# Modulation units spread over the first product and the down products, and first units of two projections loaded to places of their own, in a two-block transformer kernel

## What the reference computes, cut to what matters

```
h = h + short_conv_mixer(rms_norm(h), a_w_in, a_conv, a_w_out)      # layer 0
h = h + swiglu(rms_norm(h), f_w_gu, f_w_down)
h = h + nsa_mixer(rms_norm(h), b_w_qg, b_w_o, shared_kv(h))         # layer 1
h = h + swiglu(...)
x = rms_norm(h)
mod = silu(c) @ w_ada + b_ada        # 1024 x 6144, the modulation
sh1, sc1, g1, sh2, sc2, g2 = split(mod, 6)
h = rms_norm_2(x) * (1 + sc1) + sh1 ;  proj = h @ w_in   # "qkv" begins it
...
```

## Time and profile before

| | |
|---|---|
| median of 3 runs | 2106.3 us |
| profiled execution, its own time | 2105.22 us |
| its span | 2103.4 us |
| granted TensorE clock, mean over the span | 0.993 |
| PE busy | 2041.8 us (97%) |
| DVE busy | 1413.6 us (67%) |
| ACT busy | 947.8 us (45%) |
| POOL busy | 719.8 us (34%) |
| DMA moved | 206.15 MB, mean 98 GB/s |

### The profile page before, as it was taken

The page is one execution under the profiler, slowest core; times in us unless marked ns, Lnnn a source line. Parts: engine busy times, 40 slices in busy tenths (PEclk is TensorE's granted clock), DMA queues, the critical chain, the costliest instruction groups (busy, mean ns, idle before and its releaser), DMA issues.

```text
span 2103.4 us, 31407 instructions
## 1 busy us (share of the span) xinstructions
PE 2041.8 (97%) x12206; PEld 1732.8 (82%) x12206; DVE 1413.6 (67%) x2047; ACT 947.8 (45%) x1523; POOL 719.8 (34%) x512
## 2 busy tenths in 40 slices
PE   8988999999999999999999989999999999999999
PEld 6876899989788644789898978778778888989898
DVE  6996856838472798487592947575775748749393
ACT  4122434525332588444352545465454535435252
POOL 5663134242542311303424242322124250342333
PEclk9999999999999999999999999999999999999999
DMA  6674123232343100122323231211112122233232
GB/s 249 253 262 179 61 81 121 91 110 84 118 170 91 46 1 1 69 73 81 120 91 110 89 119 61 80 41 61 61 43 81 57 81 87 85 111 111 91 109 93
DMA packets 37722, 206.15 MB, mean 98 GB/s; under 512 B 4432, under 2 KB 5584, under 8 KB 18256
## 3 DMA queue, kind: packets, MB, share of 16 engines
q1 hardware_dynamic: 35568, 197.36, 27.4%
q10 hardware_dynamic: 2016, 6.88, 1.0%
HBM read 200.10 MB, written 2.10 MB: 96 GB/s over the span
## 4 chain that ended last, share of the span: by engine, by line
PE 65%; issue 19%; POOL 7%; DVE 6%; DMA 1%; ACT 1%; SPq 0%; POOLq 0%; DVEq 0%; ACTq 0%
PE PS L806 27%; POOL WL L531 7%; PE PS L876 5%; PE PS L877 5%; PE PS L878 5%; DVE AWC L2452 2%; PE PS L1088 2%; PE PS L1119 2%; PE PS L721 2%; PE PS L1101 2%; PE PS L722 2%; PE PS L723 2%; PE PS L655 1%; PE PS L775 1%; PE PS L776 1%
## 5 line engine op out<-in xcount | busy, mean ns | idle before, releaser
L531 POOL TENSOR_TENSOR WL<-WR,WH 128x512 fp32r<-128x512 f32 x224 | 328.2, 1496 | 543.0 <-ACT WH L1509 540.0
L588 POOL TENSOR_TENSOR LS<-WR,HS 128x512 fp32r<-128x512 f32 (+1 forms) x144 | 176.6, 1248 | 270.2 <-ACT HS L1744 270.2
L569 POOL TENSOR_TENSOR LF<-LF,WR 128x512 f32<-128x512 f32 x57 | 78.7, 1380 | 456.3 <-PE PS L806 248.1
L1509 ACT ACTIVATE WH<-WR 128x2048 fp32r<-128x2048 f32 x55 | 105.1, 1911 | 223.1 <-PE PS L723 133.1
L876 PE MATMUL PS<-G3h,HS 128*128 128x512 f32 x522 | 203.7, 390 | 0.7 <-DVE G3l L2561 0.7
L877 PE MATMUL PS<-G3l,HS 128*128 128x512 f32 x522 | 203.3, 390 | 0.0
L878 PE MATMUL PS<-G3h,LS 128*128 128x512 f32 x522 | 203.1, 389 | 0.0
L721 PE MATMUL PS<-Hh,WH 128*128 128x512 f32 x400 | 160.5, 401 | 18.1 <-POOL WL L531 10.3
L1744 ACT ACTIVATE HS<-WR 128x1024 fp32r<-128x1024 f32 (+1 forms) x72 | 71.2, 988 | 197.4 <-PE PS L878 187.4
L723 PE MATMUL PS<-Hh,WL 128*128 128x512 f32 x400 | 158.0, 395 | 0.0
L722 PE MATMUL PS<-Hl,WH 128*128 128x512 f32 x400 | 157.9, 395 | 0.0
(11 more groups left out here) (425 smaller groups left out, 4923.9 us busy)
## 6 DMA issues: line engine op xcount, KB each, us to landing
WR<-wA SPq DMA_DIRECT2D x125, 1024.0 KB, 4.8
AW<-wada SPq DMA_DIRECT2D x24, 1024.0 KB, 4.8
WR<-wD SPq DMA_DIRECT2D x48, 512.0 KB, 3.6
WR<-wE SPq DMA_DIRECT2D x24, 384.0 KB, 3.0
X<-x_in SPq DMA_DIRECT2D x8, 256.0 KB, 6.9
W1K<-w1k ACTq DMA_DIRECT2D x1, 2048.0 KB, 8.1
W1V<-w1v ACTq DMA_DIRECT2D x1, 2048.0 KB, 12.9
out<-X SPq DMA_DIRECT2D x8, 256.0 KB, 3.7
```

The costliest lines, as they stand in the source:

```text
L531: ins = nc.gpsimd.tensor_tensor(WL[:, s, piece], WR[:, s, piece], WH[:, s, piece].bitcast(F32), ALU.subtract)
L588: ins = nc.gpsimd.tensor_tensor(low[:, piece], WR[:, s, piece], high[:, piece].bitcast(F32), ALU.subtract)
```

## The change

Modulation. The 24 units are no longer done in the first product and "wout". `MODULATION` gives 6 to "win" (one behind each of the steps 1 to 6), 4 to each of dn0a, dn0b, dn1a and dn1b, and 2 to dn0c. In a down product SP waits, behind the load of unit 3, until the first tile is made, and then issues a condition row (512 KB) and two modulation units (1 MB each) ahead of the load of unit 4; the third and fourth come behind the loads of units 4 and 5. They go to `AWP`, parts of HS and LS that are free during a down product. ACT applies SiLU to the condition row behind the high part of unit 2; DVE does one unit behind each of the tiles 1 to 4 (tiles 2 and 3 in dn0c). b_ada is added in dn1b. The result of a reduction is written over its input. In dn0c the load of ACT's logarithm table comes behind that SiLU.

Direct loads. The first units of "wq" and of "qkv" are loaded into places of their own (RAWQ, RAWQ0) behind unit 5 of dn0c and dn1c, with no wait for a slot of WR; ACT makes their high part behind unit 7 (tile 5), and POOL their low part over the raw one, in one instruction of 2048 columns. `raw_loads` counts the loads of a slot without them. The second unit's high part comes last in dn0c's queue of ACT; in dn1c it moves from ahead of the norm into `norm_hi`, ahead of chunk 5.

Low products late. "wq" begins with the products that need only the high part, for all chunks of both tiles, and then waits for the low part.

```diff
+MODULATION = {"win": range(0, 6), "dn0a": range(6, 10), "dn0b": range(10, 14), "dn0c": range(14, 16),
+              "dn1a": range(16, 20), "dn1b": range(20, 24)}
+DIRECT_UNITS = [SEGS["wq"].unit0, SEGS["qkv"].unit0]
...
+        AWP = [at(f"AWP{k}", kb, [P, KMAX]) for k, kb in enumerate((166, 180, 112, 128))]
...
+            def down(name):
+                seg = SEGS[name]
+                for m in range(seg.units):
+                    load_unit(seg, m % seg.upb, m // seg.upb)
+                    if m == 3 and name in MODULATION:
+                        sp.wait_ge(tile_s, seg.tile0 + 1)
+                        load_condition(name)
+                        load_ada(MODULATION[name][0])
+                        load_ada(MODULATION[name][1])
+                    if m in (4, 5) and len(MODULATION.get(name, ())) > 2:
+                        load_ada(MODULATION[name][m - 2])
+                    if m == 5 and name in ("dn0c", "dn1c"):
+                        load_direct(("wq", "qkv")[int(name[2])], name)
...
+            seg = SEGS["win"]
+            for u in range(2, seg.units):
+                load_unit(seg, u % 2, u // 2)
+                if u in (6, 8, 9, 11):
+                    load_ada((6, 8, 9, 11).index(u) + 2)
...
+                            if both and lows_late:
+                                pe.wait_ge(hi_s, seg.unit0 + 1)
+                                for c in range(seg.chunks):
+                                    ready(c)
+                                    for m in tiles:
+                                        rows = PS[:, m, :]
+                                        nc.tensor.matmul(rows, wh[:, c, m * P:m * P + P], xh(c), start=c == 0, stop=False)
+                                        nc.tensor.matmul(rows, wh[:, c, m * P:m * P + P], xl(c), start=False, stop=False)
+                                pe.wait_ge(lo_s, seg.unit0 + 1)
...
             def norm_hi(shift):
                 for m in range(CUT, DC):
+                    if m == DC - 3:
+                        hi(SEGS["qkv"].unit0 + 1)
...
             def down_with_squares(l):
-                act.preload_act_table_set("natural_log_exp_and_others")
                 for m in range(DC):
                     if m + 2 < DC:
                         down_high(l, "c", m + 2)
-                    elif l == 1:
-                        hi(following.unit0 + m + 2 - DC)
...
+                    if m == 0:
+                        if l == 0:
+                            condition_silu("dn0c")
+                        act.preload_act_table_set("natural_log_exp_and_others")
+                    if m == DC - 2:
+                        hi(following.unit0)
                     if l == 1 and m == DC - 1:
                         break
...
                     for m in range(2, DC):
                         down_high(l, half, m)
+                        if m == 2 and l < 2:
+                            condition_silu(f"dn{l}{half}")
...
             def conv_mixer():
-                    if j:
-                        modulation_unit(t - 2)
...
-                    if j:
-                        modulation_unit(t - 1)
...
-                    modulation_unit(t)
+                    if 1 <= j <= len(MODULATION["win"]):
+                        modulation_unit("win", j - 1)
...
+                    if l < 2 and 1 <= m <= 4:
+                        modulation_unit(f"dn{l}{half}", m - 1)
...
-            residual("wout", lows={DC - 3: 0, DC - 2: 1}, cut=True, modulation=(22, 23))
+            residual("wout", lows={DC - 3: 0, DC - 2: 1}, cut=True)
...
+            residual("dn0c", next_h=(Hh, Hl, "b_norm"), modulation=MODULATION["dn0c"])
```

More of the change, by code:

```diff
@@ L130, in slot, with raw_loads, modulation_slot, modulation_loads @@
     return seven_unit(n) % 2
+MODULATION = {"win": range(0, 6), "dn0a": range(6, 10), "dn0b": range(10, 14), "dn0c": range(14, 16),
+              "dn1a": range(16, 20), "dn1b": range(20, 24)}
+DIRECT_UNITS = [SEGS["wq"].unit0, SEGS["qkv"].unit0]
+def raw_loads(u):
+    return sum(k % 2 == u % 2 and k not in (0, *DIRECT_UNITS) for k in range(u + 1))
+def modulation_slot(n):
+    return n % 2 if n < 6 else (n - 6) % 4
+def modulation_loads(n):
+    return sum(modulation_slot(k) == modulation_slot(n) for k in range(n + 1))
+def condition_rows(name):
+    return list(MODULATION).index(name) + 1
 def first_free(n):
@@ L474, in _ @@
             sp.dma_start(slopes[:, :], consts[:, C_SLOPES:C_SLOPES + NH + 1]).then_inc(const_s, 16)
-            sp.dma_start(CROW[:, :], consts[:, C_COND:C_COND + D]).then_inc(crow_s, 16)
-            for n in range(2):
-                load_ada(n, n)
-            for name in ("win", "wout"):
-                seg = SEGS[name]
-                for u in range(seg.units):
-                    if seg.unit0 + u < 2:
-                        continue
-                    load_unit(seg, u % 2, u // 2)
-                    if 4 <= seg.unit0 + u <= 14:
-                        for n in (2 * (seg.unit0 + u - 3), 2 * (seg.unit0 + u - 3) + 1):
-                            load_ada(n, n % 2)
-            for name, _, _ in SEGMENTS[2:]:
-                segment(name)
+            load_condition("win")
+            load_ada(0)
+            load_ada(1)
+            seg = SEGS["win"]
[3 more added lines that the diff above has]
+                    load_ada((6, 8, 9, 11).index(u) + 2)
+            for name, _, _ in SEGMENTS[1:]:
+                if name[:2] == "dn":
+                    down(name)
+                elif name in ("wq", "qkv"):
+                    for u in range(1, SEGS[name].units):
+                        load_unit(SEGS[name], u % 2, u // 2)
+                else:
+                    segment(name)
             for m in range(DC):
@@ L675, in body @@
                                       for x in WX[seg.unit0 + seg.upb * i + k])
-                        if not in_pieces and not (pieces is not None and first and k == 1):
+                        if not in_pieces and not (pieces is not None and first and k == 1) and not (lows_late and k == 0):
                             pe.wait_ge(lo_s, seg.unit0 + seg.upb * i + k + 1)
@@ L695, in body @@
                                 continue
+                            if both and lows_late:
[7 more added lines that the diff above has]
+                                pe.wait_ge(lo_s, seg.unit0 + 1)
+                                for m in tiles:
+                                    for c in range(seg.chunks):
+                                        last = nc.tensor.matmul(PS[:, m, :], wl[:, c, m * P:m * P + P], xh(c),
+                                                                start=False, stop=c == seg.chunks - 1)
+                                    last.then_inc(tile_s, 1)
+                                    if m == 0 and stats:
+                                        norm_stats()
+                                continue
                             lows_last = pieces is not None and first and k == 1 and tiles[0] == 0
@@ L2451, in modulation_unit @@
                 for b in range(2):
+                    half = rows[:, b * D:b * D + D]
                     ins = nc.vector.tensor_tensor_reduce(
-                        out=AWC[:, b, :], in0=AW[:, slot, b * D:b * D + D], in1=CROW[:, :], scale=1.0, scalar=0.0,
+                        out=half, in0=half, in1=condition_row(name), scale=1.0, scalar=0.0,
                         op0=ALU.mult, op1=ALU.add, accum_out=MOD[:, 2 * n + b:2 * n + b + 1])
@@ L2573, in down @@
                     ins.then_inc(evac_s, 1)
+                    if l < 2 and 1 <= m <= 4:
+                        modulation_unit(f"dn{l}{half}", m - 1)
+                    if l == 1 and half == "b" and m == 4:
+                        chain.wait()
+                        dve.wait_ge(ada_acc_s, 24)
+                        nc.vector.tensor_tensor(MOD[:, :], MOD[:, :], pcol("bada", 0, 48), ALU.add).then_inc(mod_done, 1)
                     if first is not None and m == 5:
+                        if l < 2:
+                            dve.wait_ge(ada_acc_s, MODULATION[f"dn{l}{half}"][-1] + 1)
                         sums_one_three(first)
```

105 lines of the change are left out of this document (64 added, 41 removed).

## The result

The changed kernel took 2086.46 us (median; 2085.59 to 2087.1), the kernel before 2106.88 us beside it (2106.02 to 2107.5): ratio 0.9903, 95% interval 0.9886 to 0.992. A second series on another occasion gave 2086.85 us and 0.9904 (0.9887 to 0.992). Forecast were 2088.0 us in 2080 to 2095, and "faster". The profiled execution spans 2083.8 us; before it was 2103.4, so 19.6 us of span are to be explained.

A forecast was written before the change was run, and what follows sets the result against it. PE, busy 97% of the span, was taken as the bound. 17.7 - 3.2 - 3.0 + 6.3 + 0.5 = 18.3 us off 2105.2 gave 2086.9, plus 1.1 for the median 2088.0 us; 8-in-10 range 2080 to 2095.

The forecast's parts named there:

- First product: First product and start of "wout": four PE gaps and a clock fall go; gain 17.7 us, bounds 12.2 to 17.7.
- D-type products: dn0a, dn0b, dn1a, dn1b: DVE's reductions beside POOL cost PE 0.2 us at 16 tiles; loss 3.2 us.
- dn0c: Down product dn0c: ACT's fuller queue delays unit 3's high part, PE idles; loss 3.0 us, bounds 1 to 6.
- "wq": Start of "wq": the 4.39 us gap and its half clock go; gain 6.3 us, bounds 4.4 to 6.6.
- Norm behind dn1c: PE gap there mostly stays, POOL still holding DVE's sums; net gain 0.5 us, bounds loss 1, gain 9.
- Rival A: Norm behind dn1c: gap closes, POOL's long instruction ending before DVE's last sums; 7 us more gain, 2081; chance 0.16.
- Rival B: Down products: POOL and DVE in step, or late SiLU, cost 0.5 us per tile, clock falls; 2094; chance 0.17.
- Rival C: Transfers starve down products, slower than before: unit 4 at 18.1 us (200 GB/s); 2110 us at 190 GB/s; chance 0.03.
- Rival D: First product not paced by PE: POOL's low parts still late, half of 17.7 us kept back; 2096; chance 0.07.

The follow-up runs named there:

- the fastest version: Changed kernel with modulation loads spread behind weight units, later SiLU in dn0c, and POOL's first qkv low part behind the last column sum: 2079.72 us, ratio 0.9873.

## Why the prediction was right

It gave 18.3 us; the profile shows 19.6 of span, the times 20.4. By its own steps:

- **First product: 17.7 forecast, 20.76 measured, and "at most the 17.7" was wrong.** Cause and place were right: all four gaps went, and moving the modulation back brought 21.7 us back. Two things were mis-sized. The gap lengths count from the modelled end of the matmul in front; start to start, less one step of 0.23 us, the four are 2.59 + 0.96 + 2.51 + 9.92 = 15.98 us, not 15.34. And the prediction counted only the clock fall at "wout" (2.5 us); before there was another behind the gap at 35.31 (1.5 us), which none of its rows held, and after there was not. 15.98 + 2.5 + 1.5 = 20.0; the other 0.8 is not assigned. The 1.5 us is luck of the profile and no merit of the change, as the last section shows.
- **D-type products: 3.2 forecast, 2.57 measured.** 0.56, 0.69, 0.72 and 0.60 us. The mechanism was shown: without the long reductions it is 0.00. Unit 4's load was forecast at 10.4 us and seen at 11.3, past its need at 10.9, and did not matter: with the same loads in the queue and the reductions short, the segments lost nothing.
- **dn0c: 3.0 forecast, 5.19 measured; the value taken was too small, the bound of 6 held.** The gap was 3.03 us, at the forecast tile, by the forecast queue. But the clock fell behind it (1.56 us), which stood in the bound and not in the sum, and some 0.5 us is not assigned. Its cause, ACT waiting for the condition row ahead of unit 3, is shown by six profiles with the gap 0.32 to 0.35 us under the wait, and by the run that made unit 3 first, in which the gap at this tile is gone. The row landed 4.2 us after the tile and not 3.7. What the prediction missed is that unit 4's load stood right behind as a second stall.
- **"wq": 6.3 forecast, 6.89 measured**, over the upper bound of 6.6. Of the gap of 4.39, the own place alone closes all but 0.45; the reserve of 0.3 us for the second unit was not needed.
- **Norm behind dn1c: 0.5 forecast, 1.47 measured.** POOL's instruction came at 1229.36 and held DVE's sum to its end, three more sums and the additions followed, PE resumed at 1238.34 after 5.99 us, "near 6". The 0.7 us to be given back behind it did not come: the high part of the second unit cost no gap over 0.4 us. Rival A, POOL clear of the sums, did not happen by itself; where it was made to, PE's gap shrank by 3.3 us, to 2.71, which is the chain of sums itself, and 1 us of that came back because POOL's 4.6 us then held XN. So the 7 us of that rival were not there to be had.
- **Not in the sum: 0.60 + 1.16 us lost** mostly to falls of the clock at places that the change does not touch. With the 1.5 us won near 36 the lucky and the unlucky falls nearly cancel in this profile.

The errors +3.1, +0.6, -2.2, +0.6, +1.0 and -1.8 add up to 1.3 us: that the total came so near is in part luck, since errors of up to 3.1 us in single terms offset each other. Rival B (0.5 us per tile, clock falls) got the fall in dn0c right and the price per tile wrong: 2.57 / 16 = 0.16 us. Rival C (200 GB/s) never came near: unit 4 landed 11.3 us after tile 0, not 18.1. Rival D fell with the four gaps.

By the Trainium skill (ScalarE: Activation LUTs, section "What ACT_TABLE_LOAD costs") dn0c would have lost another 1.4 us to a drain. The timeline of ACT after the change has the SiLU, the load of 1.28 us at 516.40 and the next activation at 517.70, so there is no drain here. By the Trainium skill (SBUF — State Buffer, section "A bandwidth-pool intuition that's wrong (but worth ruling out)"), with 358 GB/s for a core, the prediction's estimate had unit 4 land at 11.2 us. It did at 11.3, but the agreement is chance: the window from 12 to 27 us moved 393 GB/s, and this one, with unit 4 on its way in dn0a, moved 418 (columns as in the windows above):

```profile
286.00:293.00 7.00, 7.00 (x32) 5.65 (x31) 4.09 (x5) 2.12 (x2) 4.10 (x3) 1.00 1.01 418
```

## What to carry to other kernels

Count a load's place in the in-order queue by what stands ahead of it, and spread large side loads behind the loads that the bound engine needs: three 1 MB loads in a row behind unit 4 (two in dn0c) only moved the stall to unit 5, one behind unit 4 and two behind unit 5 removed it. When one engine's queue waits for a load and then does side work, put what feeds the bound engine first, and look for the second stall behind the first before pricing the cure. Price a gap of PE start to start and add the clock fall that may follow; a fall that appears in one profile alone belongs into the range and not into an explanation.

## What the runs showed of the hardware

- **The same gap is followed by a fall of the clock in one profile and not in the next.** In the thirteen profiles of the twelve kernels, the code up to about 36 us is almost the same, with PE gaps of 1.74 to 1.82 us there; the granted clock went to 0.50 for some 3.4 us in seven (about 1.5 us lost each time) and stayed at 1.00 in six. Behind the gap of 2.10 us that stands at 1334 in the changed kernel it fell in eight of thirteen, behind the one of 2.11 us at 1454 in six. The changed kernel's own two profiles differ. A fourth place, near 700 us, has a fall in nine of thirteen, 0.6 or 1.5 us lost. Four such places make up to 6 us between two runs of one kernel; the fastest version's times spread over 4.4 us (2076.98 to 2081.36). Length alone does not decide: the clock stayed at 1.00 behind gaps of 2.43 and 2.35 us in the kernel before and of 2.29 us in dn0c with short reductions, and fell behind one of 1.92 us with the later SiLU. Why it falls in some profiles stays open. Behind the gaps of 9.76 and 9.78 us, and behind the norm's gap of 2.71 to 7.38 us in all thirteen, it was at 0.50.
- **POOL and DVE hold each other for whole instructions, whichever starts first, but not where DVE reads PSUM.** A DVE sum of 0.68 us took 4.37 beside POOL's 4.58; moved away, an XN of 0.47 us took 3.04 in its stead. In dn0a a reduction (289.62 to 291.93) was held by a POOL piece until 290.85, and the next piece (290.80 to 293.08) by that reduction. But `X<-X,PS` at 1229.51 took its usual 0.69 us inside POOL's 4.58. The two halves of the gate in the feed-forward parts, same operation and shape, one with an operand in PSUM and one with both in SBUF, show it in the changed kernel (ns min/median/max):

```profile
L2651 DVE SCALAR_TENSOR_TENSOR HF<-SG,PS x57: 407/422/423, 238.0 to 2048.8; 128x256 f32<-128x256 f32 x57
L2654 DVE SCALAR_TENSOR_TENSOR HF<-SG,U x57: 418/1282/1416, 238.3 to 2049.2; 128x256 f32<-128x256 f32 x57
```

  Twelve of the first ran wholly inside a POOL instruction and took 0.41 to 0.42 us, as alone. The way out is to choose what is held, or to give DVE an operand in PSUM there; the latter was not tried in this kernel.
- **The 512 KB condition row, issued at the end of tile 0 of dn0c, was there 3.4 to 4.9 us later** (ACT's SiLU at 513.14 after a high part started by the same tile at 509.69, and at 517.23 after 512.36), with nothing ahead of it in the queue, and PE's gap followed one to one.
